# Inverting 32x32 triangular blocks in RWKV-7: transposes by VectorE, or a second product on TensorE

## The chip, the cores and the metric

One core of a Trainium2 chip runs the whole program. The metric is the device time of one execution in microseconds, as a median of three runs. TensorE multiplies, VectorE and ScalarE work on what it leaves in PSUM, GpSimd takes side work, and SyncE only issues the DMAs of the weights.

## What is computed

One inference step of a two-layer backbone over 128 context tokens and 256 latent tokens (384 in all, width 1024, float32). Each layer normalises, projects, runs three branches (convolution, Fourier, RWKV-7), merges them with gates, and applies a feed-forward part (dense in layer 0, top-2-of-8 experts in layer 1). The change touches the RWKV-7 branch alone. Its recurrence over time, per head of 64 channels and in both directions, is

```python
def wkv_scan(r, w, k, v, a_, b_, s0, reverse):
    def step(s, inp):
        r_t, w_t, k_t, v_t, a_t, b_t = inp
        sa = jnp.einsum("bhvk,bhk->bhv", s, a_t)
        s = (s * w_t[:, :, None, :] + sa[..., None] * b_t[:, :, None, :]
             + v_t[..., None] * k_t[:, :, None, :])
        return s, jnp.einsum("bhvk,bhk->bhv", s, r_t)
```

## The kernel before

The scan is done in chunks of C = 64 tokens, six chunks in all, held as NCP = 3 pairs (index `u` or `cp`, 128 tokens on the 128 partitions) of NH = 8 heads. Inside a chunk the terms `sa` depend on one another through a strictly triangular 64x64 matrix A, one for each chunk and head, so the kernel needs the inverse of a unit triangular matrix. It inverts the two 32x32 blocks on the diagonal (B = 32) first and joins them afterwards. This **inversion stage** runs four times in the program, once for each layer `l` and direction `d`; a run of it is called a pass here.

A pass goes as follows. TensorE computes all products of pairs of tokens (`"pair"` jobs), and VectorE masks them into `S1` (line 1672), whose columns 0 to 63 hold A. The tile `TQ` holds for every pair and head the current approximation T of the inverse in columns 0 to 31, and its transpose in columns 32 to 63. The four quarters of the partitions hold the four 32x32 blocks of a pair, and a matmul of TensorE works on one quarter: 8 heads x 4 quarters = 32 matmuls make one batch of 32x32. T begins as the unit matrix and is right for blocks of 1, 2, 4, 8 and 16 before the five levels (LEVELS = 5), each of which doubles the size: T takes the entries of T A T where the mask of the level allows it.

- Level 0 needs no product, because T is the unit matrix: VectorE copies the unit matrix into columns 32 to 63 (line 1676), copies entries of A from `S1` under the mask `level_one`, once for each half (line 1682), and transposes the result into columns 0 to 31 (line 1685).
- In levels 1 to 4, TensorE computes X from `S1` and T, one batch for each of the three pairs `u` (job `"X"`, printed as `bank<-TQ,S`). ScalarE copies X from PSUM to `Xs[u]` (line 1287). TensorE then computes T A T, again three batches (job `"TAT"`, printed as `bank<-Xs,TQ`). VectorE copies it into columns 0 to 31 under the mask (`copy_predicated`, line 1691) and transposes columns 0 to 31 into 32 to 63 (line 1693).
- At the end, the jobs `"XO"` and `"QO"` (half as many matmuls in a batch) join the two blocks, and GpSimd copies the transposes from `TQ` to `Q` (line 2003).

The order on each engine is that of the program text. On TensorE, `begin` gives each job the next of four PSUM banks in turn and waits until the job that had the bank before is drained. The waits of the steps are these: `at("T_turned", l, d, lev, u)` for VectorE's transpose of a pair, `drained(...)` for the copy out of a bank, `filled(...)` for a batch of TensorE. In a level before the change TensorE goes through X for u = 0, 1, 2 and then through TAT for u = 0, 1, 2. All matmuls go through the helper `mm`, so that the profile puts all of them on line 573 (line 567 of the changed file), and they are told apart by tiles. After the pass, the same engine runs the recurrence over chunks (jobs `"W"`, `"U"`, `"S"`), and in between products of the adaLN weights for the next layer.

The masks lie in one table in DRAM that is loaded in two parts, `first` and `second`; the level masks are in `second`.

Of the kernel before, what the change touches and what calls it, by code (L numbers as in the profile page):

```python
# [52 lines left out]
def tables():  # L53
# [28 lines left out]
    for m in range(LEVELS):  # L82
        b = 1 << m
        low = (s // (2 * b) == t // (2 * b)) & (s // b > t // b)
        if m > 0:
            lev += [low, low.T]
        else:
            none = low & False
            first_, second_ = [np.concatenate([x, none] * 2) for x in (low.T, low)], [np.concatenate([none, x] * 2) for x in (low.T, low)]
            out["level_one"] = np.concatenate([first_[0], second_[0], first_[1], second_[1]], 1)  # L90
    out["level_mask"] = np.tile(np.concatenate(lev, 1), (4, 1))
    out["eye"] = np.tile(np.eye(B), (4, 1))
# [100 lines left out]
def build(nc, dram, outs, marks):  # L193
# [4 lines left out]
    with ExitStack() as ctx:  # L198
# [122 lines left out]
        def tab(name):  # L321
            a, n = tcol[name]
            return first[:, a:a + n] if name in FIRST else second[:, a - n_first:a - n_first + n]
# [3 lines left out]
        level_mask = tab("level_mask").rearrange("p (l w) -> p l w", l=LEVELS - 1)  # L327
        level_one = tab("level_one").rearrange("p (d a w) -> p d a w", d=2, a=2)
# [36 lines left out]
        def at(name, *key):  # L365

            return sem(name).h, marks.get((name,) + key, 1)
# [180 lines left out]
        def _(pe):  # L548
# [23 lines left out]
            def mm(out, lhsT, rhs, start, stop):  # L572
                return pe.matmul(out, lhsT, rhs, start=start, stop=stop)  # L573
# [93 lines left out]
            for l in range(DEPTH):  # L667
# [81 lines left out]
                for d in range(2):  # L749
# [30 lines left out]
                    for lev in range(1, LEVELS):  # L780
                        for u in range(NCP):
                            b = begin("X", l, d, lev, u)
                            if lev == 1:
                                pe.wait_ge(*at("T_turned", l, d, 0, u))
                            else:
                                pe.wait_ge(*drained("TAT", l, d, lev - 1, u))
                            for h in range(NH):
                                for q, blk in quarters:
                                    last = mm(b[q, h * B:(h + 1) * B], S1[q, u, h, blk * B:(blk + 1) * B],
                                              TQ[q, u, h, 0:B], True, True)  # L790
                            last.then_inc(*E.fill("X", l, d, lev, u))
                        for u in range(NCP):
                            b = begin("TAT", l, d, lev, u)
                            pe.wait_ge(*at("T_turned", l, d, lev - 1, u))
                            pe.wait_ge(*drained("X", l, d, lev, u))
                            for h in range(NH):
                                for q, blk in quarters:
                                    last = mm(b[q, h * B:(h + 1) * B], TQ[q, u, h, B:C], Xs[u][q, h * B:(h + 1) * B], True, True)
                            last.then_inc(*E.fill("TAT", l, d, lev, u))

                    for u in range(NCP + 1):
# [9 lines left out]
                        if u > 0:  # L811
                            w = u - 1
                            b = begin("QO", l, d, w)
                            pe.wait_ge(*at("T_turned", l, d, LEVELS - 1, w))
# [629 lines left out]
        def _(dve):  # L1444
# [88 lines left out]
            for l in range(DEPTH):  # L1533
# [128 lines left out]
                for d in range(2):  # L1662
# [11 lines left out]
                    dve.wait_ge(*E.latest())  # L1674
                    for u in range(NCP):
                        dve.tensor_copy(TQ[:, u, :, B:C], tab("eye").rearrange("p (a w) -> p a w", a=1).broadcast_to([P, NH, B]))\
                            .then_inc(*E.step())
                    for half in range(2):
                        dve.wait_ge(*E.latest())
                        msk = level_one[:, d, half:half + 1, :].bitcast(I32).broadcast_to([P, NH, B])  # L1680
                        for u in range(NCP):
                            dve.copy_predicated(TQ[:, u, :, B:C], msk, S1[:, u, :, half * B:(half + 1) * B]).then_inc(*E.step())  # L1682
                    dve.wait_ge(*E.latest())
                    for u in range(NCP):
                        dve.transpose(TQ[:, u, :, 0:B], TQ[:, u, :, B:C]).then_inc(*E.up("T_turned", l, d, 0, u))
                    for lev in range(1, LEVELS):
                        msk = level_mask[:, lev - 1:lev, B * d:B * d + B].bitcast(I32).broadcast_to([P, NH, B])
                        for u in range(NCP):
                            dve.wait_ge(*filled("TAT", l, d, lev, u))
                            src = bank("TAT", l, d, lev, u)[:, 0:NH * B].rearrange("p (h w) -> p h w", h=NH)  # L1690
                            dve.copy_predicated(TQ[:, u, :, 0:B], msk, src).then_inc(*E.read("TAT", l, d, lev, u))
                            dve.wait_ge(*E.latest())
                            dve.transpose(TQ[:, u, :, B:C], TQ[:, u, :, 0:B]).then_inc(*E.up("T_turned", l, d, lev, u))
# [274 lines left out]
        def _(pool):  # L1968
# [10 lines left out]
            for l in range(DEPTH):  # L1979
# [14 lines left out]
                for d in range(2):  # L1994
# [3 lines left out]
                    for u in range(NCP):  # L1998
                        pool.wait_ge(*at("T_turned", l, d, LEVELS - 1, u))
# [39 lines left out]
```

## Time and profile before

| | |
|---|---|
| median of 3 runs | 2359.57 us (2357.82 to 2406.38) |
| the profiled execution | 2357.82 us |
| its span | 2356.0 us, mean granted clock 0.901 |
| TensorE busy | 1991.8 us, 85% of the span, 20096 matmul records |
| VectorE busy | 1068.6 us, 45% |
| ScalarE busy | 862.8 us, 37% |
| GpSimd busy | 860.2 us, 37% |

The span is what the profile sees between the first and the last instruction; the execution's own time is 1.8 us longer. Times in the rows are microseconds from the start of the span unless ns stands there. PE is TensorE's matmuls, PEld its weight loads, DVE is VectorE, ACT ScalarE, POOL GpSimd. A row of the timeline merges instructions of one kind that follow each other: its start, its length, the engine, line and operation, the tiles (out<-in), the count, and in brackets how long the engine had been idle and what ended it. "issue" there means that the profile shows nothing that the engine waited for.

### The profile page before, as it was taken

The numbers are of one execution on the slowest core, as the hardware profiler recorded it, in microseconds if no ns is written. First come the engines' busy times: TensorE is split into PE (matmuls) and PEld (weight loads), VectorE is DVE, ScalarE is ACT, GpSimd is POOL, SyncE is SP. The second block draws the span as 40 slices with busy tenths as digits, with TensorE's granted clock in tenths as the row PEclk, the third lists the DMA queues.
The fourth block names the chain that finished last, engine by engine and source line by source line (L and its number), as shares of the span: only waits on it lengthen the run. The fifth ranks groups of instructions, "written<-read, shape, count | busy, mean of one in ns | idle before, by whom it ended". The sixth has DMA issues, their size and how long they took to land. (4 is left out here: it accounts for less than half of the span.)

```text
span 2356.0 us, 47973 instructions
## 1 busy us (share of the span) xinstructions
PE 1991.8 (85%) x20096; PEld 1736.4 (74%) x20096; DVE 1068.6 (45%) x1434; ACT 862.8 (37%) x1287; POOL 860.2 (37%) x602
## 2 busy tenths in 40 slices
PE   4698859579998999979975948999879999999997
PEld 3497757478977999979765847887766667777675
DVE  0247332533333111024733253332267778787776
ACT  1234211213324434343421211322345556666564
POOL 0067400002433666646640000343324445454442
PEclk7599959669999999999995956999889999999999
DMA  9841006232333344433200000142267777877770
GB/s 306 264 119 61 1 4 218 91 93 79 116 107 99 117 134 122 134 107 106 65 1 4 4 2 3 48 133 91 89 246 251 257 269 273 288 260 246 245 261 33
DMA packets 225041, 315.01 MB, mean 134 GB/s; under 512 B 15584, under 2 KB 169574, under 8 KB 224742
## 3 DMA queue, kind: packets, MB, share of 16 engines
q1 hardware_dynamic: 217856, 306.22, 39.4%
q10 hardware_dynamic: 7014, 6.23, 0.9%
q8 instruction: 141, 2.31, 0.4%
q14 instruction: 30, 0.25, 0.0%
HBM read 310.31 MB, written 2.10 MB: 133 GB/s over the span
## 5 line engine op out<-in xcount | busy, mean ns | idle before, releaser
L1977 POOL TENSOR_TENSOR weights_rest<-ring,weights_rounded 128x512 fp32r<-128x512 f32 x344 | 461.8, 1344 | 625.9 <-ACT weights_rounded L1159 624.6
L190 POOL TENSOR_TENSOR e_w_rest<-e_raw,e_w_rounded 128x1024 fp32r<-128x1024 f32 (+1 forms) x108 | 276.5, 2560 | 362.8 <-ACT e_w_rounded L1399 362.8
L190 DVE TENSOR_TENSOR e_w_rest<-e_raw,e_w_rounded 128x1024 fp32r<-128x1024 f32 (+1 forms) x216 | 357.4, 1694 | 76.9 <-ACT e_w_rounded L1399 76.8
L1399 ACT ACTIVATE e_w_rounded<-e_raw 128x1024 fp32r<-128x1024 f32 (+1 forms) x324 | 314.8, 989 | 118.5 <-PE bank L573 112.4
L1159 ACT ACTIVATE weights_rounded<-ring 128x512 fp32r<-128x512 f32 x344 | 215.5, 629 | 373.6 <-PE bank L573 364.7
L573 PE MATMUL bank<-h_rounded,weights_rounded 128*128 128x384 f32 x688 | 233.4, 339 | 31.4 <-DVE h_rest L1504 31.4
L573 PE MATMUL bank<-h_rest,weights_rounded 128*128 128x384 f32 x688 | 232.5, 338 | 0.0
L573 PE MATMUL bank<-h_rounded,weights_rest 128*128 128x384 f32 x688 | 232.4, 338 | 0.0
L573 PE MATMUL bank<-e_w_rounded,hG_rounded 128*128 128x512 f32 (+1 forms) x432 | 167.1, 387 | 31.5 <-DVE e_w_rest L190 14.6
L573 PE MATMUL bank<-e_w_rounded,hG_rest 128*128 128x512 f32 (+1 forms) x432 | 161.3, 373 | 0.0
L573 PE MATMUL bank<-e_w_rest,hG_rounded 128*128 128x512 f32 (+1 forms) x432 | 161.3, 373 | 0.0
L573 PE MATMUL bank<-hg_rounded,weights_rounded 128*128 128x384 f32 x384 | 143.2, 373 | 16.1 <-DVE hg_rest L1504 11.3
L573 PEld LDWEIGHTS bank<-h_rounded,weights_rounded 128*128 128x128 f32 x688 | 131.4, 191 | 34.0 <-issue 33.2
L573 PEld LDWEIGHTS bank<-h_rest,weights_rounded 128*128 128x128 f32 x688 | 131.3, 191 | 0.0
L573 PEld LDWEIGHTS bank<-h_rounded,weights_rest 128*128 128x128 f32 x688 | 131.2, 191 | 0.0
L573 PE MATMUL bank<-hg_rest,weights_rounded 128*128 128x384 f32 x384 | 129.7, 338 | 0.0
L573 PE MATMUL bank<-hg_rounded,weights_rest 128*128 128x384 f32 x384 | 129.5, 337 | 0.0
L573 PEld LDWEIGHTS bank<-e_w_rounded,hG_rounded 128*128 128x128 f32 x432 | 81.0, 188 | 60.2 <-DVE e_w_rest L190 20.6
L573 PE MATMUL bank<-TQ,S 32*32 32x32 f32 x3456 | 63.1, 237 | 60.7 <-issue 41.1
L573 PEld LDWEIGHTS bank<-TQ,S 32*32 32x32 f32 x3456 | 57.5, 150 | 64.8 <-issue 64.8
L573 PE MATMUL bank<-ring,condp 128*32 128x128 f32 x1536 | 72.3, 350 | 36.0 <-DMA ring<-in_w_ada 36.0
L1992 POOL TENSOR_SCALAR diag<-first,vec 128x128 f32<-128x128 f32 x124 | 97.8, 805 | 13.5 <-PE bank L573 12.6
(289 smaller groups left out, 3756.8 us busy)
## 6 DMA issues: line engine op xcount, KB each, us to landing
ring<-in_w_ada SPq DMA_DIRECT2D x96, 512.0 KB, 5.8
e_raw<-in_moe_w_down SPq DMA_DIRECT2D x90, 512.0 KB, 4.9
ring<-in_w_in SPq DMA_DIRECT2D x88, 512.0 KB, 4.6
e_raw<-in_moe_w_gate SPq DMA_DIRECT2D x72, 512.0 KB, 5.5
e_raw<-in_moe_w_up SPq DMA_DIRECT2D x72, 512.0 KB, 6.1
e_raw<-in_moe_w_gate SPq DMA_DIRECT2D x36, 384.0 KB, 4.1
e_raw<-in_moe_w_up SPq DMA_DIRECT2D x36, 384.0 KB, 3.9
ring<-in_ffn_w_gate SPq DMA_DIRECT2D x22, 512.0 KB, 4.7
```

Source lines behind the costliest of these rows:

```text
L190: eng.tensor_tensor(wl, e_raw[n % E_RAW][:, 0:kn * w], wr.bitcast(F32), ALU.subtract).then_inc(s(e_rester(n)[0]), 1)
L573: return pe.matmul(out, lhsT, rhs, start=start, stop=stop)
L1159: a(w_parts[n % NSLOT][0], raw, ACT.Copy).then_inc(*E.up("rounded_ready", *key))
L1399: a(e_w[n % E_PARTS][0][:, 0:kn * w], e_raw[n % E_RAW][:, 0:kn * w], ACT.Copy).then_inc(s("e_rounded"), 1)
L1977: pool.tensor_tensor(wl, raw, wr.bitcast(F32), ALU.subtract).then_inc(*E.up("rest_ready", *key))
L1992: pool.tensor_scalar(diag[i % 8], ident, v("dw_w", l, 2 * j + m), None, ALU.mult)\
```

## The change

Level 0 is now done by TensorE like the others. The unit matrix is copied into both halves of `TQ` at once (`eye2`), which is signalled as `TQ_ready`; TensorE computes for level 0 the block of A and its transpose from `S1` and the unit matrix, without X. In levels 1 to 4, TAT computes two products in a job: T A T into the first 32 columns of a head's share of the bank and, by exchanging the two operands, its transpose into the second 32. VectorE copies both with one `copy_predicated` of 64 columns for each head, and all its transposes and the semaphore `T_turned` are gone. The order in a level is changed too: X and TAT are interleaved, TAT of pair u - 1 after X of pair u. The masks carry a further copy (`low, low.T, low`), for 5 levels in place of 4. The diff, cut to its core:

```diff
-        if m > 0:
-            lev += [low, low.T]
...
+        lev += [low, low.T, low]
...
-                    for lev in range(1, LEVELS):
-                        for u in range(NCP):
-                            b = begin("X", l, d, lev, u)
...
-                        for u in range(NCP):
-                            b = begin("TAT", l, d, lev, u)
-                            pe.wait_ge(*at("T_turned", l, d, lev - 1, u))
-                            pe.wait_ge(*drained("X", l, d, lev, u))
-                            for h in range(NH):
-                                for q, blk in quarters:
-                                    last = mm(b[q, h * B:(h + 1) * B], TQ[q, u, h, B:C], Xs[u][q, h * B:(h + 1) * B], True, True)
-                            last.then_inc(*E.fill("TAT", l, d, lev, u))
+                    for lev in range(LEVELS):
+                        for u in range(NCP + 1):
+                            if lev == 0:
...
+                                b = begin("TAT", l, d, lev, u)
+                                pe.wait_ge(*at("TQ_ready", l, d, u))
+                                for h in range(NH):
+                                    for q, blk in quarters:
+                                        mm(b[q, h * C:h * C + B], S1[q, u, h, blk * B:(blk + 1) * B], TQ[q, u, h, 0:B],
+                                           True, True)
+                                    for q, blk in quarters:
+                                        last = mm(b[q, h * C + B:(h + 1) * C], TQ[q, u, h, 0:B],
+                                                  S1[q, u, h, blk * B:(blk + 1) * B], True, True)
...
+                            if u < NCP:
+                                b = begin("X", l, d, lev, u)
...
+                            if u > 0:
+                                w = u - 1
+                                b = begin("TAT", l, d, lev, w)
+                                pe.wait_ge(*drained("X", l, d, lev, w))
+                                for h in range(NH):
+                                    for q, blk in quarters:
+                                        mm(b[q, h * C:h * C + B], TQ[q, w, h, B:C], Xs[w][q, h * B:(h + 1) * B], True, True)
+                                    for q, blk in quarters:
+                                        last = mm(b[q, h * C + B:(h + 1) * C], Xs[w][q, h * B:(h + 1) * B], TQ[q, w, h, B:C],
+                                                  True, True)
...
-                            pe.wait_ge(*at("T_turned", l, d, LEVELS - 1, w))
...
                     for u in range(NCP):
-                        dve.tensor_copy(TQ[:, u, :, B:C], tab("eye").rearrange("p (a w) -> p a w", a=1).broadcast_to([P, NH, B]))\
-                            .then_inc(*E.step())
...
+                        dve.tensor_copy(TQ[:, u, :, :], tab("eye2").rearrange("p (a w) -> p a w", a=1).broadcast_to([P, NH, C]))\
+                            .then_inc(*E.up("TQ_ready", l, d, u))
...
-                            dve.copy_predicated(TQ[:, u, :, 0:B], msk, src).then_inc(*E.read("TAT", l, d, lev, u))
-                            dve.wait_ge(*E.latest())
-                            dve.transpose(TQ[:, u, :, B:C], TQ[:, u, :, 0:B]).then_inc(*E.up("T_turned", l, d, lev, u))
...
+                            dve.copy_predicated(TQ[:, u, :, :], msk, src).then_inc(*E.read("TAT", l, d, lev, u))
...
-                        pool.wait_ge(*at("T_turned", l, d, LEVELS - 1, u))
+                        pool.wait_ge(*drained("TAT", l, d, LEVELS - 1, u))
```

On TensorE, at the start of the first pass, the program before has level 1's three X batches and three TAT batches in this row, each a batch of 32 (the numbers at the names are those of buffers; `S1_82` is `S1`, `TQ_78` is `TQ`):

```order
L573 MATMUL bank3<-TQ_78,S1_82 32x32 x32
L573 MATMUL bank0<-TQ_78,S1_82 32x32 x32
L573 MATMUL bank1<-TQ_78,S1_82 32x32 x32
L573 MATMUL bank2<-Xs0_110,TQ_78 32x32 x32
L573 MATMUL bank3<-Xs1_111,TQ_78 32x32 x32
L573 MATMUL bank0<-Xs2_112,TQ_78 32x32 x32
```

In the changed program, level 0 stands there first, three batches of 64. The rows below are the end of its last one and the beginning of level 1, up to the second TAT:

```order
L567 MATMUL bank1<-TQ_78,S1_82 32x32 x4
L567 MATMUL bank1<-S1_82,TQ_78 32x32 x4
L567 MATMUL bank2<-TQ_78,S1_82 32x32 x32
L567 MATMUL bank3<-TQ_78,S1_82 32x32 x32
L567 MATMUL bank0<-Xs0_110,TQ_78 32x32 x4
L567 MATMUL bank0<-TQ_78,Xs0_110 32x32 x4
...
L567 MATMUL bank1<-TQ_78,S1_82 32x32 x32
L567 MATMUL bank2<-Xs1_111,TQ_78 32x32 x4
L567 MATMUL bank2<-TQ_78,Xs1_111 32x32 x4
```

The two rows of four stand eight times in each TAT, once for each head. The X batch of pair 2 now comes after the TAT of pair 0.

On VectorE at the same place, the program before masks the pair products and then prepares level 0, after which each pair has its predicated copy and its transposition:

```order
L1672 TENSOR_TENSOR S_82<-bank,second 128x2x256 x12
L1676 COPY TQ<-second 128x8x32 x3
L1682 COPY_PREDICATED TQ<-second,S_82 128x8x32 x6
L1685 STREAM_TRANSPOSE TQ<-TQ 128x8x32 x3
L1691 COPY_PREDICATED TQ<-second,bank 128x8x32
L1693 STREAM_TRANSPOSE TQ<-TQ 128x8x32
```

The changed program has the whole pass in two rows there, ahead of the copies of `QO` into `Q`:

```order
L1681 TENSOR_TENSOR S_82<-bank,second 128x2x256 x12
L1684 COPY TQ<-second 128x512 x3
L1691 COPY_PREDICATED TQ<-second,bank 128x512 x15
L1697 COPY Q<-bank 32x8x32 x6
L1703 MEMSET St 128x512
```

Nothing but the three copies is left between the masking and the first matmul of the stage, and the 15 copies out of the banks are twice as wide.

## Rows read from the trace of the kernel before

**Rows 1.** The page: busy time and share of the span, by engine
```profile
PE 1991.8 (85%) x20096; PEld 1736.4 (74%) x20096; DVE 1068.6 (45%) x1434; ACT 862.8 (37%) x1287; POOL 860.2 (37%) x602
```

**Rows 2.** Stretches: us; busy PE, PEld, DVE, ACT, POOL; PEclk, DMA share, GB/s
```profile
301.00:346.00 45.00, 24.16 (x1584) 22.69 (x1586) 10.73 (x26) 4.77 (x13) 0.00 (x0) 0.50 0.02 4
346.00:365.00 19.00, 18.13 (x337) 16.18 (x333) 4.44 (x10) 4.04 (x10) 3.27 (x4) 0.62 0.16 48
365.00:420.00 55.00, 47.39 (x993) 40.12 (x993) 20.45 (x35) 10.55 (x19) 0.00 (x0) 0.95 0.77 250
451.00:496.00 45.00, 22.86 (x1443) 21.49 (x1444) 10.14 (x24) 4.22 (x11) 0.00 (x0) 0.50 0.02 4
1247.00:1292.00 45.00, 25.15 (x1600) 23.53 (x1592) 10.38 (x24) 5.60 (x15) 2.02 (x3) 0.50 0.02 4
1390.00:1435.00 45.00, 24.29 (x1584) 22.71 (x1581) 10.71 (x26) 4.78 (x13) 1.76 (x3) 0.50 0.02 5
```

**Rows 3.** Waits, 298 to 352 us: us in total, times, longest
```profile
PE bank L573 <- issue: 21.3, 12, 2.1
...
PE bank L573 <- DVE TQ L1685: 4.9, 1, 4.9
```

**Rows 4.** Timeline of the first pass: start us, us, engine line op, count [idle before]
```profile
290.01 7.27 DVE L1672 TENSOR_TENSOR S<-bank,second 128x512 f32<-128x512 f32 x12 [4.71 <-PE bank L573]
...
297.32 0.71 DVE L1676 COPY TQ<-second 128x256 f32<-128x256 f32 x3
298.06 2.26 DVE L1682 COPY_PREDICATED TQ<-second,S 128x256 f32<-128x256 int32 x6
300.36 1.10 DVE L1685 STREAM_TRANSPOSE TQ<-TQ 128x256 f32<-128x256 f32 x3
...
300.95 2.81 PE L573 MATMUL bank<-TQ,S 32*32 32x32 f32 x192 [4.91 <-DVE TQ L1685]
302.09 0.38 ACT L1287 ACTIVATE Xs<-bank 128x256 f32<-128x256 f32 x1 [12.51 <-PE bank L573]
...
303.53 0.86 PE L573 MATMUL bank<-Xs,TQ 32*32 32x32 f32 x45
...
305.92 1.93 PE L573 MATMUL bank<-Xs,TQ 32*32 32x32 f32 x127 [1.53 <-issue]
...
309.62 0.48 PE L573 MATMUL bank<-Xs,TQ 32*32 32x32 f32 x19 [1.77 <-issue]
...
309.92 1.62 PE L573 MATMUL bank<-TQ,S 32*32 32x32 f32 x104
...
313.60 1.33 PE L573 MATMUL bank<-TQ,S 32*32 32x32 f32 x83 [2.05 <-issue]
```

**Rows 5.** DMA queues, 301 to 346 us: packets, MB, share
```profile
q8 instruction: 12, 0.20, 2.1%
```

**Rows 6.** Timeline of TensorE, starts of blocks in the four passes
```profile
344.48 0.48 PE L573 MATMUL bank<-Xs,TQ 32*32 32x32 f32 x19 [2.00 <-issue]
...
456.31 2.04 PE L573 MATMUL bank<-Xs,TQ 32*32 32x32 f32 x127 [1.93 <-issue]
...
494.95 0.37 PE L573 MATMUL bank<-Xs,TQ 32*32 32x32 f32 x11 [2.03 <-issue]
...
1254.54 1.20 PE L573 MATMUL bank<-Xs,TQ 32*32 32x32 f32 x71 [1.74 <-issue]
...
1291.04 0.53 PE L573 MATMUL bank<-TQ,S 32*32 32x32 f32 x13 [1.15 <-issue]
...
1396.80 1.66 PE L573 MATMUL bank<-Xs,TQ 32*32 32x32 f32 x108 [1.58 <-issue]
...
1433.93 0.80 PE L573 MATMUL bank<-TQ,S 32*32 32x32 f32 x23 [1.85 <-issue]
```

**Rows 7.** DMA issues, 0 to 120 us: queue, count, KB, us to landing
```profile
second<-in_tables ACTq DMA_DIRECT2D x1, 1488.0 KB, 12.8
```

**Rows 8.** Instructions that read the tables: ns min/median/max, first and last start us
```profile
L573 PE MATMUL bank<-ksq,second x16: 519/845/847, 206.1 to 1155.5; 128*128 128x384 f32 x16
```

More of the change, by code:

```diff
@@ L84, in tables @@
         low = (s // (2 * b) == t // (2 * b)) & (s // b > t // b)
-        if m > 0:
-            lev += [low, low.T]
[L87 to L90, printed above, removed]
+        lev += [low, low.T, low]
     out["level_mask"] = np.tile(np.concatenate(lev, 1), (4, 1))
-    out["eye"] = np.tile(np.eye(B), (4, 1))
+    out["eye2"] = np.tile(np.eye(B), (4, 2))
     out["reset"] = np.tile(np.arange(T) % C != 0, (P, 1))
@@ L326, in build @@
         pair_mask = tab("pair_mask").rearrange("p (d w) -> p d w", d=2)
-        level_mask = tab("level_mask").rearrange("p (l w) -> p l w", l=LEVELS - 1)
-        level_one = tab("level_one").rearrange("p (d a w) -> p d a w", d=2, a=2)
+        level_mask = tab("level_mask").rearrange("p (l w) -> p l w", l=LEVELS)
         time_p = tab("time_p").rearrange("p (j k n) -> p j k n", j=1, k=2)
@@ new lines, in _ @@
+                    for lev in range(LEVELS):
+                        for u in range(NCP + 1):
+                            if lev == 0:
+                                if u == NCP:
+                                    continue
+                                b = begin("TAT", l, d, lev, u)
[7 more added lines that the diff above has]
+                                                  S1[q, u, h, blk * B:(blk + 1) * B], True, True)
+                                last.then_inc(*E.fill("TAT", l, d, lev, u))
+                                continue
+                            if u < NCP:
+                                b = begin("X", l, d, lev, u)
+                                pe.wait_ge(*drained("TAT", l, d, lev - 1, u))
+                                for h in range(NH):
+                                    for q, blk in quarters:
+                                        last = mm(b[q, h * B:(h + 1) * B], S1[q, u, h, blk * B:(blk + 1) * B],
+                                                  TQ[q, u, h, 0:B], True, True)
+                                last.then_inc(*E.fill("X", l, d, lev, u))
+                            if u > 0:
+                                w = u - 1
+                                b = begin("TAT", l, d, lev, w)
+                                pe.wait_ge(*drained("X", l, d, lev, w))
+                                for h in range(NH):
+                                    for q, blk in quarters:
+                                        mm(b[q, h * C:h * C + B], TQ[q, w, h, B:C], Xs[w][q, h * B:(h + 1) * B], True, True)
+                                    for q, blk in quarters:
+                                        last = mm(b[q, h * C + B:(h + 1) * C], Xs[w][q, h * B:(h + 1) * B], TQ[q, w, h, B:C],
+                                                  True, True)
+                                last.then_inc(*E.fill("TAT", l, d, lev, w))
@@ L1672, in _ @@
                             tt(S1[:, cp, h0:h0 + 3:2, :], src, msk, M).then_inc(*E.read("pair", l, d, cp, hp))
-                    dve.wait_ge(*E.latest())
                     for u in range(NCP):
-                        dve.tensor_copy(TQ[:, u, :, B:C], tab("eye").rearrange("p (a w) -> p a w", a=1).broadcast_to([P, NH, B]))\
-                            .then_inc(*E.step())
[L1678 to L1687, printed above, removed]
+                        dve.tensor_copy(TQ[:, u, :, :], tab("eye2").rearrange("p (a w) -> p a w", a=1).broadcast_to([P, NH, C]))\
+                            .then_inc(*E.up("TQ_ready", l, d, u))
+                    for lev in range(LEVELS):
+                        msk = level_mask[:, lev:lev + 1, B * d:B * d + C].bitcast(I32).broadcast_to([P, NH, C])
                         for u in range(NCP):
                             dve.wait_ge(*filled("TAT", l, d, lev, u))
-                            src = bank("TAT", l, d, lev, u)[:, 0:NH * B].rearrange("p (h w) -> p h w", h=NH)
-                            dve.copy_predicated(TQ[:, u, :, 0:B], msk, src).then_inc(*E.read("TAT", l, d, lev, u))
-                            dve.wait_ge(*E.latest())
-                            dve.transpose(TQ[:, u, :, B:C], TQ[:, u, :, 0:B]).then_inc(*E.up("T_turned", l, d, lev, u))
+                            src = bank("TAT", l, d, lev, u)[:, :].rearrange("p (h w) -> p h w", h=NH)
+                            dve.copy_predicated(TQ[:, u, :, :], msk, src).then_inc(*E.read("TAT", l, d, lev, u))
                     dve.wait_ge(*at("Q_zero", l, d))
```

8 lines of the change are left out of this document (removed).

## The prediction

> **What bounds the kernel now.** I read the page's shares first, because they say which engine is long. TensorE is busy for 85% of the span and VectorE for 45% [rows 1]. The change sits in one stage, the inversion of the triangular blocks, which runs four times. So I next asked for busy time by stretch, 45 us inside each of the four passes [rows 2]. The reader is to see four things there. TensorE is busy only 23 to 25 of the 45 us. VectorE is busy some 10 us and ScalarE 4 to 6, so neither is long. GpSimd does nothing but its copy at the end of a pass. The DMA engines are at 0.02 of their time, since the ring of weights is full. Nothing runs beside the stage that could take in a delay or profit from one: whatever TensorE's own line gains or loses here, the span gains or loses.
>
> Why is TensorE idle for nearly half of it? The waits of the first pass name "issue", time in which no semaphore was awaited: 21.3 us in 12 pieces. VectorE's transposition before the start is awaited once, 4.9 us [rows 3]. The timeline shows the shape of these pieces [rows 4]. From 300.95 us, 192 matmul records run in 2.81 us, which is 14.6 ns each. Two records are one matmul of the code: the 192 are the three batches X of level 1, with 32 matmuls each, and every 32x32 matmul in float32 is recorded twice, beside as many weight loads. Then come blocks of 127 records. One starts at 305.92, is over in 1.93 us, and TensorE stands still until 309.62. The next is 127 again, 19 + 3 + 1 + 104 records of two different batches (the rows of three and of one stand between the two that are shown), and then it stands still until 313.60. The cut falls in the middle of a batch whose matmuls wait for nothing. 127 matmuls and 127 weight loads are 254 instructions. The DMA view shows what comes in such portions: in the 45 us of this pass the only traffic is the instruction queue's, 12 packets in 0.20 MB, so 16 KB each and one every 3.75 us [rows 5]. I read this as: TensorE executes a block of 127 records in under 2 us and waits for the next 16 KB of its program, which arrives some 3.8 us after the last.
>
> The Trainium skill, Runtime: NRT & Kernel Launch, section Instruction fetch mechanics, says that instructions come in blocks of 16 KiB, 256 of them. The size of the packets agrees with it. It also says that the cost of crossing a block is mostly hidden, and the idle rows of 1.5 to 2.1 us after every 127 records speak against that here. By the page the added matmuls would cost their execution alone; that sum is the first rival.
>
> **The price of a block.** In each pass I take the start of one block after a stall and that of the tenth after it [rows 4, 6]: 305.92 to 344.48, 456.31 to 494.95, 1254.54 to 1291.04, 1396.80 to 1433.93. A tenth of each is 3.86, 3.86, 3.65 and 3.71 us; the mean is 3.77. Single blocks inside lie between 3.4 and 4.0 us (in these rows 3.70 and 3.98); a block of 127 records executes in 1.93, so the price does not depend on what TensorE does with it so long as its work is below that.
>
> **What the change adds on TensorE.** Level 0 is new there: three batches TAT of 64 matmuls, 192. In each of the levels 1 to 4 the batch X stays at 32 matmuls, and TAT grows from 32 to 64 because the transposed product is computed too: 3 x 32 x 4 = 384. Together 576 matmuls in a pass, 1152 records, 1152 / 127 = 9.07 blocks. At the four prices: 9.07 x (3.86 + 3.86 + 3.65 + 3.71) = 136.8 us. With all blocks at 3.44 it would be 125 us, with all at 3.98 it would be 144. I take the mean of rows, since forty blocks were averaged for it.
>
> **What it removes ahead of TensorE.** Before, VectorE's last masking of the pair products ends at 297.28 (290.01 + 7.27). Then come three copies of the unit matrix (0.71), six predicated copies (2.26) and three transpositions, and the first matmul starts at 300.95 when the first of these is through [rows 4]. Now the first matmul waits for one copy of 128x512. No row has this copy. The smaller one takes 0.71 / 3 = 0.24 us by its share of the row; the masking with the same 128x512 output takes 7.27 / 12 = 0.61. I take 0.45, so TensorE starts at about 297.85 and gains 3.1 us (2.9 to 3.3), 12.4 us in four passes. Is the early start worth its full length, if the program arrives so slowly? The first stall comes only after 237 records (192 + 45), so that much was there and waiting. A block is asked for when TensorE has moved on, so the chain of blocks shifts with the start. I count it in full; at worst nothing of it counts, and the sum is 12 us higher.
>
> **What it moves and what costs nothing.** VectorE loses 15 transpositions (1.10 / 3 = 0.37 us each) and 6 of its predicated copies in a pass, gets 3 others, and each now is of 128x512 in place of 128x256. The old one takes 2.26 / 6 = 0.38 us [rows 4]; the wide one lies between that and twice it, 0.75. The next level's first batch asks for it only after 160 other matmuls, 320 records or 2.5 blocks, over 9 us later. So VectorE is covered at either end; without that cover it would cost up to 0.38 us more at each of 60 places, 23 us. ScalarE's copy Xs takes 0.38 us [rows 4] and has the next X batch (64 records, 0.9 us even without a stall) between it and its reader: TAT follows X by one, so it is not waited for. The order of banks holds no new wait either. A batch comes four batches after the last user of its bank, and the drain of that user is asked for at least one batch earlier. At the end of a pass, GpSimd's copies wait for the last predicated copy in place of the transposition; 0.37 us goes, up to 0.38 comes. The table of masks grows by 128 columns, 64 KB. The table's load of 1488 KB takes 12.8 us, so 0.6 us more [rows 7], under the adaLN weights at the start: its first reader on TensorE starts at 206.1 us [rows 8]. Nothing.
>
> **The sum.** The profiled execution took 2357.8 us around a span of 2356.0. 2357.8 + 136.8 - 12.4 = 2482.2 us. The median of the runs, 2359.6, is 1.8 above that execution, so I say 2483. About 2%, 47 us, is what can be told from no change here.
>
> **The rivals.**
> First, the fetch is hidden for what is added: blocks come as fast as they are used, and the stalls have another cause that does not grow with the count. Then 4608 records cost 14.6 ns each, 67 us, and with the 12.4 gained the time is 2413. For it: 237 records did run without a stall. Against it: the blocks of 127 in all four passes and the packets at the same distance.
> Second, the side on which the kernel is not slower: the pauses are round trips between TensorE, ScalarE and VectorE (a matmul's end, a copy, a semaphore), charged to "issue" for want of a better name, and the interleaving of X and TAT with twice the matmuls in between hides them. A pass would then be pure execution from the start, 2688 records x 14.6 ns = 39.2 us, against 44.0 (300.95 to 344.96), and starts 3.1 earlier: 7.9 us less, 32 in all, 2328 us. It decides for this side if the matmuls run without pauses, because the added execution (1152 x 14.6 ns = 16.8 us in a pass) is then less than the 21.3 us of pauses that go. For it: the first X batch of a level does wait on the previous level. Against it: pauses inside batches, and none named after an engine.
> Third, the clock. TensorE's granted clock is 0.50 in the four stretches, 0.62 in the 19 us after the first pass, and 0.95 from there [rows 2]: the lower level of 1.2 GHz while TensorE idles half the time, and full speed again some 9 us after the pass. If the longer stretch delays the return by as much again, 9 us of work at half speed costs 4.5 us more in each pass, 18 in all: 2501. For it: nothing, except that the half-idle stretch is 1.8 times as long. Against it: the return followed a run of dense matmuls, and that code does not change. The small matmuls themselves take the same at either level, as the time of a block is set elsewhere.
>
> **How the numbers follow.** Forecast 0.86 (own range 2468 to 2496, from 125 and 144 us for the blocks and 12.4 or less for the start, with some room for the fetch elsewhere falling out differently), first rival 0.04, second 0.04, third 0.05, and 0.01 for something that makes it faster. The range 2464 to 2502 holds the forecast and the third. The first rival is still slower by over 2% (2.3%), the second is within it: slower 0.95, same 0.04, faster 0.01.
>
> **What would show it.** Right: in the new timeline the blocks of 127 records at 3.7 to 3.9 us go on through level 0 and all others; a pass takes about 79 us from first X or TAT to last, not 44; "issue" before TensorE grows to about 40 us a pass; nine instruction packets more in each; TensorE starts 3 us earlier after the last masking; VectorE and ScalarE keep idle. Wrong: pieces longer than 127 records without a pause, a pass of under 60 us, or pauses charged to VectorE's predicated copy or ScalarE's Xs, each over a microsecond.

## The result, and the profile after

The changed kernel takes 2493.9 us at the median of four runs (2479.3 to 2518.2), the kernel before 2358.7 (2357.4 to 2406.4). The ratio is 1.060, with a 95% interval of 1.054 to 1.065: slower by 6%. The ratio rests on all 23 executions of the changed kernel on record (2479.3 to 2529.3, median 2504.5) and the four of the kernel before, without those that are over 1.5% longer than the fastest of their kernel (five and one). The profiled execution has a span of 2484.3 us, 128.3 us more than before.

The stretches that answer to [rows 2], inside the four passes and behind the first one (us; busy time of PE, PEld, DVE, ACT and POOL; granted clock, DMA share, GB/s):

```profile
301.00:346.00 45.00, 23.11 (x1528) 21.49 (x1528) 5.80 (x8) 3.06 (x8) 0.00 (x0) 0.50 0.02 4
378.00:397.00 19.00, 18.53 (x345) 16.59 (x346) 6.24 (x14) 2.69 (x6) 1.35 (x2) 0.69 0.28 91
397.00:452.00 55.00, 46.42 (x930) 38.94 (x928) 19.24 (x31) 11.41 (x19) 0.00 (x0) 0.93 0.74 241
484.00:529.00 45.00, 22.98 (x1495) 21.54 (x1499) 5.81 (x8) 3.06 (x8) 0.00 (x0) 0.50 0.02 4
1310.00:1355.00 45.00, 22.39 (x1478) 20.92 (x1481) 5.81 (x8) 2.68 (x7) 0.00 (x0) 0.50 0.02 4
1488.00:1533.00 45.00, 25.06 (x1656) 23.32 (x1655) 6.41 (x9) 3.06 (x8) 0.00 (x0) 0.50 0.02 5
```

45 us of a pass look as they did before: TensorE busy for 22 to 25 of them, the clock at its lower level, hardly any transfers (4 to 5 GB/s). VectorE has become nearly idle, 6 us in place of 10 to 11. What has changed is how long this lasts. The wait of GpSimd, which stands between its zeroing of `Q` and the last step of VectorE on `TQ` in a pass (before, the transposition; now, the predicated copy), measures all four passes (the wait's total and its count; first of the kernel before, then of the changed one, whose first row is the wide predicated copy with its minimum, median and maximum in ns):

```profile
  POOL Q L2003: 193.8, 4
```

```profile
L1691 DVE COPY_PREDICATED TQ<-second,bank x60: 722/725/734, 298.3 to 1558.9; 128x512 f32<-128x512 int32 x60
...
  POOL Q L2001: 317.9, 4
```

This stretch is 317.9 / 4 = 79.5 us long in place of 48.5: 124.1 us more in all, of the 128.3 by which the span grew. The waits of the first pass (294 to 382 us) and the instruction packets in 79.2 us of it (296.8 to 376) answer to [rows 3, 5]:

```profile
PE bank L567 <- issue: 38.5, 21, 2.2
...
PE bank L567 <- DVE TQ L1684: 1.9, 1, 1.9
```

```profile
q8 instruction: 21, 0.34, 1.9%
```

TensorE's pauses without a releaser are 38.5 us in 21 pieces, where 21.3 us in 12 stood. There are 21 packets of its program in the 79.2 us, one in 3.77, as there was one in 3.75 before. The page counts 141 packets for the whole span before and 177 now:

```profile
q8 instruction: 141, 2.31, 0.4%
```

```profile
q8 instruction: 177, 2.90, 0.5%
```

Those are 36 packets more, 9 for each pass. The start of the first pass answers to [rows 4]:

```profile
288.92 7.27 DVE L1681 TENSOR_TENSOR S<-bank,second 128x512 f32<-128x512 f32 x12 [4.69 <-PE bank L567]
...
296.11 1.23 DVE L1684 COPY TQ<-second 128x512 f32<-128x512 f32 x3
...
296.82 0.23 PE L567 MATMUL bank<-TQ,S 32*32 32x32 f32 x5 [1.88 <-DVE TQ L1684]
```

TensorE starts at 296.82, 0.63 us after the last masking (288.92 + 7.27 = 296.19), where it had been 3.67 us; the other three passes have the same two lags. And the blocks of the four passes, the first start after a pause and a late one in each, answer to [rows 6]:

```profile
301.27 0.21 PE L567 MATMUL bank<-S,TQ 32*32 32x32 f32 x1 [1.50 <-issue]
...
374.36 0.27 PE L567 MATMUL bank<-Xs,TQ 32*32 32x32 f32 x3 [2.17 <-issue]
...
481.01 0.32 PE L567 MATMUL bank<-S,TQ 32*32 32x32 f32 x3 [2.24 <-issue]
...
557.61 0.28 PE L567 MATMUL bank<-Xs,TQ 32*32 32x32 f32 x5 [2.19 <-issue]
...
1311.23 0.21 PE L567 MATMUL bank<-TQ,S 32*32 32x32 f32 x1 [2.11 <-issue]
...
1388.79 0.69 PE L567 MATMUL bank<-TQ,S 32*32 32x32 f32 x17 [1.33 <-issue]
...
1488.01 0.21 PE L567 MATMUL bank<-S,TQ 32*32 32x32 f32 x1 [1.76 <-issue]
...
1560.79 1.44 PE L567 MATMUL bank<-TQ,S 32*32 32x32 f32 x47 [1.94 <-issue]
```

There are 19 blocks between the first two rows and 20 between those of each other pass: 3.85, 3.83, 3.88 and 3.64 us for one. The blocks hold 127 or 128 records each.

### The profile page after: what moved, and what is told of

It is laid out like the page before. It is cut to its first block and busy times, and to the rows that moved or that the text cites. A ratio compares the mean times of both kernels' runs of the same rounds, so it can differ in the third digit from the quotient of the medians.

```text
span 2484.3 us, 57129 instructions
## 1 busy us (share of the span) xinstructions
PE 2062.5 (83%) x24704; PEld 1801.3 (73%) x24704; DVE 1058.7 (43%) x1362; ACT 862.9 (35%) x1287; POOL 860.9 (35%) x602
## 5 line engine op out<-in xcount | busy, mean ns | idle before, releaser
L185 POOL TENSOR_TENSOR e_w_rest<-e_raw,e_w_rounded 128x1024 fp32r<-128x1024 f32 (+1 forms) x108 | 277.0, 2565 | 362.8 <-ACT e_w_rounded L1408 362.8
L1691 DVE COPY_PREDICATED TQ<-second,bank 128x512 f32<-128x512 int32 x60 | 43.5, 726 | 269.9 <-PE bank L567 269.9
L567 PE MATMUL bank<-TQ,Xs 32*32 32x32 f32 x3456 | 108.4, 237 | 42.6 <-issue 41.5
L567 PE MATMUL bank<-Xs,TQ 32*32 32x32 f32 x3072 | 96.5, 236 | 50.2 <-issue 50.2
L567 PE MATMUL bank<-TQ,S 32*32 32x32 f32 x4224 | 87.3, 234 | 58.3 <-issue 50.8
L567 PEld LDWEIGHTS bank<-TQ,Xs 32*32 32x32 f32 x3456 | 98.6, 151 | 44.1 <-issue 44.1
```

What stands on the lines that cost most here:

```text
L185: eng.tensor_tensor(wl, e_raw[n % E_RAW][:, 0:kn * w], wr.bitcast(F32), ALU.subtract).then_inc(s(e_rester(n)[0]), 1)
L1691: dve.copy_predicated(TQ[:, u, :, :], msk, src).then_inc(*E.read("TAT", l, d, lev, u))
```

## The experiments

All experiments are edits of the kernel before, unless something else is said. Times of a kernel vary between its executions by 25 us and more (below, under what was not expected); the executions of the kernel before that were made beside these runs have medians of 2382, 2387 and 2375 us, where the expectations speak of 2358. So the waits of GpSimd in the profile, which cover the passes alone, are given beside the ratio.

### Only the order of X and TAT

```diff
-                        for u in range(NCP):
-                            b = begin("X", l, d, lev, u)
...
-                        for u in range(NCP):
-                            b = begin("TAT", l, d, lev, u)
+                        for u in range(NCP + 1):
+                            if u < NCP:
+                                b = begin("X", l, d, lev, u)
...
+                            if u > 0:
+                                w = u - 1
+                                b = begin("TAT", l, d, lev, w)
```

> The kernel before, with the changed order alone: TAT of pair u-1 after X of pair u. Theory (TensorE waits for the next 16 KB of its program, 127 matmul records of this size at 3.8 us): the instruction count is the same, so no change, within 10 us of 2358. Rival (the pauses are round trips of data that interleaving hides): the 21.3 us of pauses in a pass shrink, down to 2328 for all that interleaving could give.

Measured: ratio 1.000 (0.994 to 1.006), medians 2382.5 us and, for the kernel before beside it, 2381.9. GpSimd's wait for the four passes is 187.2 us:

```profile
  POOL Q L2005: 187.2, 4
```

That is 6.6 us under before. The pauses of the first pass are 18.4 us in 12 pieces, as many pieces as before, with blocks a little quicker in coming. So the pauses are not round trips that this order hides, and the interleaving is worth nothing that can be measured in the time.

### The second product alone

```diff
+                                    mm(b[q, 256 + h * B:256 + (h + 1) * B], Xs[u][q, h * B:(h + 1) * B], TQ[q, u, h, B:C], True, True)
+                                for q, blk in quarters:
                                     last = mm(b[q, h * B:(h + 1) * B], TQ[q, u, h, B:C], Xs[u][q, h * B:(h + 1) * B], True, True)
```

> The kernel before, with the second product of TAT computed into unused columns of the bank and read by nobody; VectorE keeps its transpositions. 384 matmuls more in a pass, 768 records, 6.05 blocks. Theory: 6.05 x (3.86 + 3.86 + 3.65 + 3.71) = 91 us more, 2449. Rival one (fetch hidden, execution alone): 3072 records x 14.6 ns = 45 us more, 2403. Rival two (pauses are round trips): the added work fills pauses, at most 20 us more, 2378.

Measured: ratio 1.046 (1.035 to 1.058), median 2471 us against 2382 of the kernel before, lowest 2454.9 against 2353.5. The profiled span is 2453.1 us, 97 above that of before. GpSimd's wait is 277.0 us and the page counts 165 packets:

```profile
  POOL Q L2005: 277.0, 4
```

```profile
q8 instruction: 165, 2.70, 0.5%
```

1536 matmuls more in the program bring 24 packets and lengthen the passes by 83.2 us, 3.5 us for a packet. The 91 us of the theory lie between that and the 97 of the span. Of the other 14 us some 10 lie in the recurrence behind the fourth pass, which takes 60.6 us here, from `St` set to zero to the copy of the last state, and 50.7 in the kernel before; in its first 38 us the granted clock is 0.60 where it was 0.88. Execution alone, 45 us, falls short of 83 and of 97. The added products wait for nothing new and nobody waits for their results.

### X over twice as many columns

```diff
-                                    last = mm(b[q, h * B:(h + 1) * B], S1[q, u, h, blk * B:(blk + 1) * B],
-                                              TQ[q, u, h, 0:B], True, True)
+                                    last = mm(b[q, h * C:(h + 1) * C], S1[q, u, h, blk * B:(blk + 1) * B],
+                                              TQ[q, u, h, :], True, True)
```

> The kernel before, with every X matmul run over 64 columns in place of 32 (both halves of TQ, the second result unused): the same number of instructions, more execution in each. X also waits for the transposition now. Theory: a block of 127 records executes in under 3 us and still takes 3.8 us to come, so no change, within 12 us of 2358. Rival one (execution sets the pace): 1536 matmuls take 29 ns more each, 45 us more, 2403.

Measured: ratio 1.003 (0.997 to 1.009). GpSimd's wait is 190.2 us. The group of the wider X, by form (busy us, mean ns | idle before it):

```profile
  POOL Q L2000: 190.2, 4
```

```profile
L573 PE MATMUL bank<-TQ,S 32*32 32x64 f32 x3072 | 79.0, 282 | 34.9 <-DVE TQ L1682 19.7 <-issue 15.2
```

3072 records of 64 columns are there. They fill the pauses with their own length: before these records and those of the joining step 15.2 + 4.6 us of idle time without a releaser are left, where the page of the kernel before has 41.1 us. So a pause is no fixed price of a block that comes on top of its execution: it is the rest of some 3.8 us that the block's execution does not fill. Execution can be added for nothing until it fills them. This run and the one before tell the two causes apart: more instructions cost, more columns up to that point do not.

The run settles one more rival, that the blocks are slow because TensorE's clock is at its lower level. With the longer matmuls the granted clock is higher in the passes, 0.76 in the first where it was 0.50:

```profile
300.00:346.00 46.00, 28.98 (x1628) 27.45 (x1631) 10.82 (x27) 6.10 (x16) 1.15 (x2) 0.76 0.02 4
```

The blocks come no faster for it: ten of them lie between the starts at 309.38 and 346.85 us of that pass, 3.75 us for one.

### No transpositions

```diff
                             dve.copy_predicated(TQ[:, u, :, 0:B], msk, src).then_inc(*E.read("TAT", l, d, lev, u))
-                            dve.wait_ge(*E.latest())
-                            dve.transpose(TQ[:, u, :, B:C], TQ[:, u, :, 0:B]).then_inc(*E.up("T_turned", l, d, lev, u))
```

The waits for these transpositions, of TensorE and GpSimd, become waits for the predicated copy.

> The kernel before without VectorE's transpositions of levels 1 to 4; the second half of TQ keeps its values of level 0, so the inverse is not computed to its end. It shows what the change could win at most by taking the transpositions away. Theory: nothing waits for them, so no change, within 8 us of the kernel before. Rival (pauses are round trips through VectorE): 48 transpositions of 0.44 us go, 21 us if each is on the path, up to 32 if TensorE's pauses close too.

Measured: ratio 1.000 (0.995 to 1.005), medians 2384 us and 2387, and GpSimd's wait is 193.1 us where it was 193.8:

```profile
  POOL Q L2001: 193.1, 4
```

These 48 of the 60 transpositions that the change takes away were wholly hidden, and taking them away can win nothing in this kernel. The other 12 are those of level 0; TensorE did wait for the first of each pass, and that is part of the earlier start.

### The change with level 0 left to VectorE

```diff
-                    for lev in range(LEVELS):
+                    for lev in range(1, LEVELS):
...
-                        dve.tensor_copy(TQ[:, u, :, :], tab("eye2").rearrange("p (a w) -> p a w", a=1).broadcast_to([P, NH, C]))\
-                            .then_inc(*E.up("TQ_ready", l, d, u))
...
+                        dve.transpose(TQ[:, u, :, 0:B], TQ[:, u, :, B:C]).then_inc(*E.up("T_turned", l, d, 0, u))
```

The diff is against the changed kernel; the steps of level 0 are those of the kernel before.

> The changed kernel, but level 0 prepared by VectorE as before; TAT's second product, the wide predicated copy and the interleaving stay. 384 matmuls more than before in a pass in place of 576, and TensorE starts no earlier than before. Theory (the count of instructions): the same 6.05 blocks as in e2, so 91 us over the kernel before, ratio 1.039, within 8 us of what e2 gave over its own before (97). If level 0 on TensorE were what costs most, this would be near the kernel before.

Measured: ratio 1.034 (1.018 to 1.050), lowest 2438.7 us against 2354.2, 84.5 more. GpSimd's wait is 283.1 us:

```profile
  POOL Q L2004: 283.1, 4
```

89.3 us over before, where 83.2 was measured for the second product alone and 91 expected. The passes so agree with that run to 6 us. The lowest executions do not meet the expectation of 97 within 8, since 10 of those 97 us were the longer recurrence told of there. (The profile is that of an execution of 2502 us, in which the recurrences behind the third and the fourth pass take 75 us each in place of 51; the wait covers the passes alone.) So the second product costs 83 to 89 us of the change's 124, and level 0 on TensorE the remaining 35 (317.9 - 283.1): 768 matmuls, 12.1 blocks, 46 us by the price of a block, less the 12 us of the earlier start. Level 0 by itself is a loss too.

### Half the instructions for the same inverse

T and its transpose are held as block-diagonal 64x64 matrices, so that each matmul does the work of two. The zeros outside the diagonal blocks make the product right, and the masks are as wide.

```diff
-                            for h in range(NH):
-                                for q, blk in quarters:
-                                    last = mm(b[q, h * B:(h + 1) * B], S1[q, u, h, blk * B:(blk + 1) * B],
-                                              TQ[q, u, h, 0:B], True, True)
+                            for h in range(NH):
+                                for q in pairs_:
+                                    last = mm(b[q, h * C:(h + 1) * C], S1[q, u, h, 0:C], TQ[q, u, h, :], True, True)
...
+                                    last = mm(b[q, h * C:(h + 1) * C], Q[q, u, h, :], Xs[u][q, h * C:(h + 1) * C], True, True)
...
+                            dve.transpose(Q[:, u, :, :], TQ[:, u, :, :]).then_inc(*E.up("T_turned", l, d, lev, u))
```

> Half the instructions for the same inverse: T and its transpose are kept as block-diagonal 64x64 (TQ and Q), so that one 64x64 matmul does what two of 32x32 did; levels 1 to 4 have 96 matmuls each in place of 192, and GpSimd's copy into Q is gone. Copies of ScalarE and VectorE are twice as wide. Theory: 6.05 blocks fewer in a pass, up to 91 us less, 2267; if the larger matmuls' execution or VectorE's wide copies take over as the bound, about half of that, 2310. Rival one (execution sets the pace; a 64x64 record of 128 columns took 37.3 ns against 14.6, one of 64 columns some 25): 768 x 25 = 19.2 us against 22.4 in a pass, 13 us less, 2345.

Measured: ratio 0.972 (0.961 to 0.982), median 2313.0 us against 2381.9, lowest 2286.0 against 2353.5. It is faster, but by less than 2% at the upper end of the interval. The page counts 117 packets, 24 fewer than before:

```profile
q8 instruction: 117, 1.92, 0.4%
```

One level of the first pass in its timeline:

```profile
300.61 4.94 PE L570 MATMUL bank<-TQ,S 64*64 64x64 f32 x96 [5.24 <-DVE TQ L1680]
...
311.08 3.00 PE L570 MATMUL bank<-Xs,Q 64*64 64x64 f32 x96
...
312.25 0.73 DVE L1686 COPY_PREDICATED TQ<-second,bank 128x512 f32<-128x512 int32 x1 [1.52 <-PE bank L570]
313.02 0.71 DVE L1688 STREAM_TRANSPOSE Q<-TQ 128x512 f32<-128x512 f32 x1
313.66 0.69 DVE L1686 COPY_PREDICATED TQ<-second,bank 128x512 f32<-128x512 int32 x1
...
313.88 3.13 PE L570 MATMUL bank<-TQ,S 64*64 64x64 f32 x96
...
315.05 0.60 ACT L1283 ACTIVATE Xs<-bank 128x512 f32<-128x512 f32 x1 [3.14 <-PE bank L570]
```

TensorE goes from one batch to the next without a pause, 3.00 and 3.13 us for the 96 records of a level's TAT and X, and VectorE keeps up with it (0.7 us each). A level takes some 5.7 us where it took 11.7 (384 records at 3.86 us for 127). From the last masking to the start of the recurrence the four passes take 141.4 us in place of 221.3, 80 less. Behind the first X, no row of TensorE in the levels stands behind a pause, so the pass is now bound by execution as far as the profile shows, and the gain of 68 us between the lowest executions, 69 between the medians, lies between the 91 and the 48 that were expected. The two ends of the same theory are so seen: with more instructions slower, with fewer faster.

### The same, started earlier

```diff
+                    for u in range(NCP):
+                        pool.tensor_copy(Q[:, u, :, :], tab("eye").rearrange("p (a w) -> p a w", a=1).broadcast_to([P, NH, C]))\
+                            .then_inc(*E.up("Q_unit", l, d, u))
```

> As e6_blocks_of_64, with the unit matrices copied by GpSimd while VectorE still masks, and level 0 done pair by pair, so that TensorE's first X starts some 1.5 to 2.7 us earlier in each of four passes. In e6 TensorE is busy 28.4 of 30 us in a pass and has no pauses for its program, so an early start counts in full: 6 to 11 us under e6, some 75 under the kernel before, ratio 0.968.

Measured: ratio 0.971 (0.959 to 0.983), median 2300.5 us, lowest 2283.5, 2.6 under the lowest of the version without it; its profiled span is 2281.6. The start of the first pass:

```profile
295.66 1.72 POOL L1987 COPY Q<-second 128x512 f32<-128x512 f32 x3 [34.49 <-PE bank L570]
296.86 1.09 DVE L1674 COPY_PREDICATED Q<-second,S 128x512 f32<-128x512 int32 x1
297.99 0.71 DVE L1676 STREAM_TRANSPOSE TQ<-Q 128x512 f32<-128x512 f32 x1
...
298.84 1.44 PE L570 MATMUL bank<-TQ,S 64*64 64x64 f32 x22 [3.27 <-DVE TQ L1676]
```

VectorE masks until 296.82, and TensorE's first X starts 2.0 us later, where it was 4.0 us in the version before this one. The 1.09 us of the first predicated copy, 0.4 longer than the next, lies beside GpSimd's copies. The start came earlier as planned; that it brings the 6 us is not shown, since the executions differ by more.

### Without the fillers

TensorE runs filler matmuls (`FILL = 4`) in the recurrence behind a pass where the adaLN products have run out. They were taken out of the kernel before and out of the version just told.

```diff
-FILL = 4
+FILL = 0
```

> The kernel before without the filler matmuls (FILL = 0) that keep TensorE busy in the recurrence behind a pass, in layer 1 and wherever the adaLN products have run out. It asks what the granted clock costs behind a pass. Theory of the clock: after a pass at the lower level TensorE gets the upper level back only after a stretch of unbroken work, which the fillers give; without them the recurrences of layer 1 stay at the lower level, 5 to 20 us more each, less the fillers' own time of up to 12 us each: between 2350 and 2375. Rival (the clock does not matter there, since the recurrence waits for ScalarE and VectorE): the time falls by the fillers' share, to 2340.

> As e7_blocks_of_64_early, without the fillers. There the pass itself runs without pauses, at 0.90 of the clock in its profile, so the recurrence starts at the upper level. Theory of the clock: it is lost or kept by what the recurrence does alone; between 10 us faster and 10 us slower than e7. Rival: 15 us faster than e7, as in the other kernel.

Measured: for the kernel before a ratio of 1.001 (0.998 to 1.005), 2373.8 us at the median and between 2370 and 2377 in nine of ten executions. For the early version a ratio to the kernel before of 0.967 (0.959 to 0.975), median 2283.2 us, lowest 2280.8. In the kernel before, the rival of 2340 falls: nothing is won against 2375, the median of the kernel before beside it, as the theory of the clock had it; what the clock does there is told in the last section. The early version without fillers is the fastest of this study, some 3% under the kernel before. Against the version with the fillers, which was run at another time, its gain is not resolved: the medians, 2283 and 2300, speak for the rival (15 us faster), the lowest, 2281 and 2283, for the theory of the clock.

## Why the prediction was right

The direction was right, the median of 2493.9 us lies in the range of 2464 to 2502, and it is 11 us above the 2483 that was forecast. The ratio of 1.060 on 2358.7 gives 2499.5, which is 17 us above it and still in the range. That the time itself fell into the range owes something to luck. The forecast started from 2359.6 us, which is near the fast end of the kernel before: over all 49 executions of it on record the median is 2382.0. And over all 23 executions of the changed kernel the median is 2504.5, 2.5 us above the range. The difference between the kernels does not hang on this: it is 122.5 us between these medians and 125.8 between the lowest times (2479.3 and 2353.5), and 136.8 - 12.4 = 124.4 was forecast. Step by step:

**What bounds the stage.** Right, and now shown by edits and not only by a shape in the timeline. More instructions cost (second product alone, 24 packets, 83 us in the passes), more execution at the same count costs nothing, another order nothing, no transpositions nothing, half the matmuls gains. The packets' own times in the trace of the kernel before fit the prediction's "a block is asked for when TensorE has moved on": in the first pass blocks start at 305.92, 309.62, 313.60 and 317.57 us and packets at 307.08, 310.82, 314.83 and 318.80, each some 1.2 us later; a packet takes 1.2 to 1.3 us, only one is under way at a time, and TensorE goes on 1.4 to 1.5 us after it. The statement of the Trainium skill, Runtime: NRT & Kernel Launch, section Instruction fetch mechanics, that a crossing is mostly hidden does not hold here for blocks of 32x32 matmuls, which execute in 1.9 us and then stand still. It does hold in the version with 64x64 matmuls, where 127 records would execute in some 4 us (an estimate from 96 in 3.00 to 3.13): no pause for the program is left in its levels.

**The price and count of blocks.** 136.8 us was the term. The passes grew by 124.1 us in GpSimd's wait, and TensorE began 3.04 us earlier in each, so the blocks cost 124.1 + 12.2 = 136.3. The count was 9.07 and 9 packets a pass were seen. The four prices, 3.85, 3.83, 3.88 and 3.64, were taken as 3.86, 3.86, 3.65 and 3.71. The price is not that exact from one profile to another: in the run with the order alone it was 3.60 to 3.74 us and with the second product alone 3.64 to 3.68, so that the term met its measurement to under 1 us is luck.

**The earlier start.** 3.1 us was said, 3.04 measured; it did count in full.

**VectorE's wide copy.** 0.725 us, near the upper end of 0.38 to 0.75, and hidden. The 0.38 was read too low: it divides the length of a row by six copies that overlap, and a single copy of the old width lasts 0.44 us. Nothing depended on it.

**The first and second rival** fell, the first by the second product's run (83 us in the passes, not 45), the second by the new order and by the missing transpositions.

**The third rival**, that the clock returns later behind a pass, was given 0.05 and 4.5 us a pass. The profile of the changed kernel does not show it: 0.69 in the 19 us behind the first pass, 0.93 after that. Other profiles show a clock that returns late behind a pass at about five times that price, in the kernel without transpositions and in the version with 64x64 matmuls as well, whose passes are no longer than before. It was mis-sized, then, and it is not a property of the change alone. The sum of the forecast meets the executions without it: 2482.2 against 2479.3, 2482.3 and the profiled one, 2486.1. The executions at 2505 and 2518 lie 20 to 35 us higher, and they pull the median of the four up to 2493.9. No trace of them was kept, but their mean granted clock is on record: 0.870 and 0.865, where those at 2479 and 2482 have 0.880 and 0.881. The kernel before has the same steps (0.900 at 2357, 0.889 at 2383), and the two medians above lie as far apart as the two lowest times, so nothing shows that the late return falls to the changed kernel more often.

## What to carry to other kernels

Before work is moved to an idle-looking engine, ask what its idle time is made of: small matmuls in long unrolled code can be paced by the program's own arrival, and then each added instruction has a price (here 3.8 us for 254), while added columns are free until they fill that time. The sign is equal counts of records between pauses without a releaser, and packets of one size in the instruction queue at the same distance. The remedy that worked here is fewer and larger instructions, even if they multiply zeros; taking work from another engine that nobody waits for wins nothing.

## What was not expected of the hardware

The granted clock can stay at its lower level for 50 us and more of a recurrence behind a pass, although TensorE works there without a gap. The stretch 1310 to 1360 us lies for the most part in the recurrence behind the third pass, here for the kernel before, for the one without transpositions and for the one without fillers, each with the start of the recurrence (`St` set to zero) and the row of its copies of Y, whose last number is the start of the last of them:

```profile
1310.00:1360.00 50.00, 42.42 (x629) 36.48 (x623) 19.97 (x34) 10.31 (x17) 0.00 (x0) 0.94 0.02 4
...
1296.51 0.48 DVE L1705 MEMSET St<- 128x512 f32 x1 [0.17 <-issue]
...
L1314 ACT ACTIVATE Y<-bank x6: 597/597/598, 400.5 to 1347.1; 128x512 f32<-128x512 f32 x6
```

```profile
1310.00:1360.00 50.00, 50.00 (x402) 45.56 (x402) 11.85 (x25) 1.94 (x4) 0.00 (x0) 0.50 0.00 1
...
1301.06 0.48 DVE L1703 MEMSET St<- 128x512 f32 x1 [0.17 <-issue]
...
L1314 ACT ACTIVATE Y<-bank x6: 597/598/600, 402.8 to 1376.2; 128x512 f32<-128x512 f32 x6
```

```profile
1310.00:1360.00 50.00, 45.74 (x561) 40.47 (x559) 12.08 (x26) 7.61 (x14) 0.00 (x0) 0.61 0.02 4
...
1298.28 0.48 DVE L1705 MEMSET St<- 128x512 f32 x1 [0.17 <-issue]
...
L1314 ACT ACTIVATE Y<-bank x6: 597/597/598, 402.1 to 1355.1; 128x512 f32<-128x512 f32 x6
```

The clock is at 0.94 in the first, and the recurrence takes 50.6 us (1296.5 to 1347.1). It is at 0.50 in the second with TensorE busy for all of the 50 us, and the recurrence takes 75.1 us. What came before is alike in both, a pass at the lower level (0.50). Without fillers TensorE is busy 45.7 of 50 us, the clock is at 0.61, and the recurrence takes 56.8 us. The steps of some 25 us between executions of one kernel (2357 and 2382 before) have this size. The expectation for the run without fillers, that their absence would keep the clock low and cost time, held in this stretch, against the first of the three. But the fillers win little on the whole: where the clock stays low in spite of them, the recurrence is the longest of the three, and the medians with and without them are the same. The 64x64 version shows it too, behind its fourth pass, though that pass (1343 to 1373 us) ran at the upper level for most of its time:

```profile
1343.00:1373.00 30.00, 28.40 (x964) 27.86 (x962) 18.87 (x30) 9.70 (x19) 0.00 (x0) 0.95 0.02 4
1373.00:1432.00 59.00, 58.77 (x455) 53.28 (x454) 12.90 (x28) 3.75 (x8) 0.00 (x0) 0.50 0.01 1
```

Its recurrence runs at 0.50 for 59 us, with 455 matmul records; the kernel before has as many (463) over in 38 us at 0.88:

```profile
1440.00:1478.00 38.00, 37.48 (x463) 33.95 (x462) 13.00 (x28) 4.02 (x8) 0.00 (x0) 0.88 0.01 2
```

So a dense pass ahead does not keep the clock up either. What decides it was not found.
